# Down-projections of a split-precision transformer: two three-step products against one 512-column and one 256-column step

## The reference

```
def swiglu_2(x, w_gate, w_up, w_down):
    return (jax.nn.silu(x @ w_gate) * (x @ w_up)) @ w_down
...
for l in range(DEPTH):
    h = rmsnorm(x, ffn1_norm[l])
    x = x + 0.5 * swiglu_2(h, ffn1_w_gate[l], ffn1_w_up[l], ffn1_w_down[l])
    ...                                    # mixer, output projection
    h = rmsnorm(x, ffn2_norm[l])
    x = x + 0.5 * swiglu_2(h, ffn2_w_gate[l], ffn2_w_up[l], ffn2_w_down[l])
return rmsnorm(x, final_norm)
```

## Time and profile before

| | |
|---|---|
| median of three runs | 1949.19 us |
| profiled execution, first to last instruction | 1945.9 us |
| TensorE busy | 1931.2 us, 99% |
| VectorE busy | 1431.5 us, 74% |
| ScalarE busy | 1019.8 us, 52% |
| mean granted TensorE clock | 0.999 |
| DMA queue of the weights | 48.0% of 16 engines |

### The profile page before, as it was taken

How to read it: one execution, slowest core, us unless ns; L and a number is a source line. 1 busy time by engine, 2 the same in 40 slices (tenths; PEclk the granted TensorE clock), 3 DMA queues, 4 the chain that set the end, 5 groups by cost and what they waited for, 6 DMA issues and landing times.

```text
span 1945.9 us, 42335 instructions
## 1 busy us (share of the span) xinstructions
PE 1931.2 (99%) x16150; PEld 1892.7 (97%) x16150; DVE 1431.5 (74%) x2591; ACT 1019.8 (52%) x1527; POOL 152.7 (8%) x192
## 2 busy tenths in 40 slices
PE   9999999999999999999999999999999999999998
PEld 8999989999999999899999999999999999999998
DVE  6774787987588768879978874667765775667763
ACT  4443687554455447865547443665445444565443
POOL 0001123000100011320010100000000000100000
PEclk9999999999999999999999999999999999999999
DMA  7454433545454544345553665445555555435554
GB/s 265 172 197 170 166 109 112 192 174 193 156 192 172 196 164 145 109 152 194 201 191 140 235 233 183 151 149 185 193 214 177 195 202 208 152 131 195 194 213 154
DMA packets 46830, 346.66 MB, mean 178 GB/s; under 512 B 5344, under 2 KB 6416, under 8 KB 9232
## 3 DMA queue, kind: packets, MB, share of 16 engines
q1 hardware_dynamic: 44416, 335.63, 48.0%
q0 software_dynamic: 2320, 9.74, 1.6%
HBM read 344.29 MB, written 1.07 MB: 177 GB/s over the span
## 4 chain that ended last, share of the span: by engine, by line
PE 91%; DVE 4%; ACT 2%; DVEq 1%; issue 1%; DMA 0%; ACTq 0%; SPq 0%; POOL 0%
PE ps L622 22%; PE ps L623 22%; PE ps L624 22%; PE ps L639 14%; PE ps L630 2%; PE ps L631 2%; PE ps L632 2%; DVE w_lo L1996 1%; PE ps L1162 0%; DVE pj L2465 0%; DMA h<-in_hidden 0%; DVE cst L2486 0%; PE ps L1197 0%; DVE pj L2462 0%; ACT scratch L1669 0%
## 5 line engine op out<-in xcount | busy, mean ns | idle before, releaser
L1996 DVE TENSOR_TENSOR w_lo<-raw,w_hi 128x1024 fp32r<-128x1024 f32 (+1 forms) x582 | 749.3, 1313 | 151.1 <-ACT w_hi L1300 91.5
L622 PE MATMUL ps<-x_hi,w_lo 128*128 128x256 f32 (+3 forms) x2208 | 622.1, 282 | 1.5 <-DVE x_lo L2087 0.6
L624 PE MATMUL ps<-x_hi,w_hi 128*128 128x256 f32 (+3 forms) x2208 | 615.1, 279 | 0.0
L623 PE MATMUL ps<-x_lo,w_hi 128*128 128x256 f32 (+3 forms) x2208 | 614.8, 278 | 0.0
L1297 ACT ACTIVATE w_hi<-raw 128x1024 fp32r<-128x1024 f32 x454 | 466.3, 1052 | 92.5 <-PE ps L639 49.0
L622 PE MATMUL ps<-hid_hi,w_lo 128*128 128x256 f32 (+1 forms) x1536 | 431.5, 281 | 0.1
L624 PE MATMUL ps<-hid_hi,w_hi 128*128 128x256 f32 (+1 forms) x1536 | 430.2, 280 | 0.0
L623 PE MATMUL ps<-hid_lo,w_hi 128*128 128x256 f32 (+1 forms) x1536 | 429.8, 280 | 0.0
L622 PEld LDWEIGHTS ps<-x_hi,w_lo 128*128 128x128 f32 x2208 | 414.9, 188 | 6.4 <-issue 4.2
L623 PEld LDWEIGHTS ps<-x_lo,w_hi 128*128 128x128 f32 x2208 | 415.0, 188 | 0.5
L624 PEld LDWEIGHTS ps<-x_hi,w_hi 128*128 128x128 f32 x2208 | 414.6, 188 | 0.0
(11 more groups left out here) (351 smaller groups left out, 2315.3 us busy)
## 6 DMA issues: line engine op xcount, KB each, us to landing
raw<-in_w_up SPq DMA_DIRECT2D x176, 1024.0 KB, 4.8
raw<-in_w_down SPq DMA_DIRECT2D x64, 1408.0 KB, 6.0
raw<-in_w_in SPq DMA_DIRECT2D x36, 1024.0 KB, 4.8
raw<-in_w_out SPq DMA_DIRECT2D x16, 1024.0 KB, 4.8
cst<-row_copy POOLq DMA_DIRECT2D x2, 1088.0 KB, 8.5
raw<-in_w_up SPq DMA_DIRECT2D x4, 512.0 KB, 7.2
cst<-in_consts POOLq DMA_DIRECT2D x1, 1537.5 KB, 6.5
prm<-in_prm POOLq DMA_DIRECT2D x2, 690.0 KB, 7.2
```

The costliest lines, as they stand in the source:

```text
L622: mm(dst, low, xa, start=first, stop=False)
L623: mm(dst, high, xb, start=False, stop=False)
L624: return mm(dst, high, xa, start=False, stop=last)
L1996: v.tensor_tensor(dst, src, high.bitcast(F32), ALU.subtract).then_inc(lo_done, 1)
```

## The change

In stages 4 to 7 the two products with the high weights become one step. The moving operand of that step is both halves of a chunk, 2 x 256 = 512 columns, and its output is a whole PSUM bank: columns 0 to 255 get high by high, columns 256 to 511 high by low. The step with the low weights (256 columns, high activations) adds into columns 256 to 511. Each f so takes two steps in place of three, with the same number of columns, 768.

VectorE adds the bank's two halves to `h` in two instructions with a drain between (`resid_halves`), in place of one.

Order and places differ by stage (`WIDE`): in stage 5 the wide step comes first for each f, in 4, 6 and 7 second (but for f = 0, where it clears the bank). In stages 4 and 5 the halves lie where they lay; in stage 6 the high and low chunks alternate, so that the 512 columns are contiguous; in stage 7 the low half lies 16 elements earlier. The two hidden buffers become one allocation, 32 elements longer. Stages 0 to 3 are as they were.

```diff
-        HID_HI_W, HID_LO_W = NF * T1 + 4 * LINE, NF * T1 + LINE
+        HID_HI_W, HID_LO_W = NF * T1 + 4 * LINE, NF * T1 + 3 * LINE
...
-        def hid_of(T):
+        FIRST_HIGH, SECOND_HIGH, ADJACENT = "high weights first", "high weights second", "halves side by side"
+        WIDE = {4: (SECOND_HIGH, 0), 5: (FIRST_HIGH, 0), 6: (ADJACENT, 0), 7: (SECOND_HIGH, LINE)}
+
+        def hid_halves(q):
+            kind, more = WIDE[q]
+            if kind == ADJACENT:
+                return hid_all[:, HID_HI_T2:HID_HI_T2 + 2 * NF * T2].rearrange("p (k e t) -> p e k t", k=NF, e=2)
+            span = HID_HI_W + HID_LO_T2 - HID_HI_T2 - more
+            both = hid_all[:, HID_HI_T2:HID_HI_T2 + 2 * span].rearrange("p (e w) -> p e w", e=2)
+            return both[:, :, 0:NF * T2].rearrange("p e (k t) -> p e k t", k=NF)
...
             def down(q, turn0, resid, T):
+                def wide(j, f, high, low):
+                    kind, _ = WIDE[q]
+                    halves, bank = hid_halves(q)[:, :, f, :], ps[:, 4 + j, :]
+                    pair = bank.rearrange("p (e t) -> p e t", e=2)
+                    if kind == FIRST_HIGH or f == 0:
+                        mm(pair, high, halves, start=f == 0, stop=False)
+                        return mm(bank[:, T2:2 * T2], low, halves[:, 0, :], start=False, stop=f == NF - 1)
+                    mm(bank[:, T2:2 * T2], low, halves[:, 0, :], start=False, stop=False)
+                    return mm(pair, high, halves, start=False, stop=f == NF - 1)
...
+                                if q in WIDE:
+                                    last = wide(j, f, high, low)
+                                else:
+                                    last = three(ps[:, 4 + j, 0:T], high, low, ha[:, f, 0:T], hb[:, f, 0:T],
+                                                 f == 0, f == NF - 1)
...
+            def resid_halves(m, bank):
+
+                c = slice(m, m + 1) if isinstance(m, int) else bass.ds(m, 1)
+                dst = h[:, c, T1 - T2:T1]
+                v.tensor_tensor(dst, dst, ps[:, bank:bank + 1, T2:2 * T2], ALU.add)
+                dve.drain()
+                v.tensor_tensor(dst, dst, ps[:, bank:bank + 1, 0:T2], ALU.add).then_inc(resid_ready, 1)
...
-                        resid(alpha, it * 2 + j, 4 + j, T)
+                        resid_halves(it * 2 + j, 4 + j)
...
-                        resid(1.0, it * 2 + j, 4 + j, T2)
+                        resid_halves(it * 2 + j, 4 + j)
```

More of the change, by code:

```diff
@@ L234, in build @@
         small = sb("small", [P, 96])
-        HID_HI_W, HID_LO_W = NF * T1 + 4 * LINE, NF * T1 + LINE
+        HID_HI_W, HID_LO_W = NF * T1 + 4 * LINE, NF * T1 + 3 * LINE
         HID_HI_T2, HID_LO_T2 = 3 * LINE, LINE
-        hid_hi_all = sb("hid_hi", [P, HID_HI_W], F32R)
-        hid_lo_all = sb("hid_lo", [P, HID_LO_W], F32R)
+        hid_all = sb("hid", [P, HID_HI_W + HID_LO_W], F32R)
+        hid_hi_all, hid_lo_all = hid_all[:, 0:HID_HI_W], hid_all[:, HID_HI_W:HID_HI_W + HID_LO_W]
         SCRATCH = HID_HI_W + HID_LO_W
@@ L305, in cat1, with hid_of @@
             return x_of(T)
-        def hid_of(T):
+        FIRST_HIGH, SECOND_HIGH, ADJACENT = "high weights first", "high weights second", "halves side by side"
[7 more added lines that the diff above has]
+            return both[:, :, 0:NF * T2].rearrange("p e (k t) -> p e k t", k=NF)
+        def hid_of(T, q):
+            if q in WIDE:
+                both = hid_halves(q)
+                return both[:, 0, :, :], both[:, 1, :, :]
             return (hidt_hi, hidt_lo) if T == T2 else (hid_hi, hid_lo)
@@ L813, in down @@
             def down(q, turn0, resid, T):
-                ha, hb = hid_of(T)
+                ha, hb = hid_of(T, q)
+                def wide(j, f, high, low):
[7 more added lines that the diff above has]
+                    return mm(pair, high, halves, start=False, stop=f == NF - 1)
                 def turn(it):
@@ L826, in turn @@
                                 col = u * W_WIDE + c * P
-                                last = three(ps[:, 4 + j, 0:T], w_hi[:, j, col:col + P], w_lo[:, j, col:col + P],
-                                             ha[:, f, 0:T], hb[:, f, 0:T], f == 0, f == NF - 1)
+                                high, low = w_hi[:, j, col:col + P], w_lo[:, j, col:col + P]
+                                if q in WIDE:
+                                    last = wide(j, f, high, low)
+                                else:
+                                    last = three(ps[:, 4 + j, 0:T], high, low, ha[:, f, 0:T], hb[:, f, 0:T],
+                                                 f == 0, f == NF - 1)
                             last.then_inc(unit_used, 1)
@@ L1335, in first_cast @@
                 src = pj[:, j:j + 1, 0:T] if it == 0 else prod[:, j:j + 1, 0:T]
-                fn(hid_of(T)[0][:, f, 0:T], src, ACT.Copy).then_inc(first_casts, 1)
+                fn(hid_of(T, 2 * DEPTH)[0][:, f, 0:T], src, ACT.Copy).then_inc(first_casts, 1)
             def up(q, turn0, T, crossing=False, place=TIGHT):
@@ L1517, in pair @@
                     f = slice(f, f + 1) if isinstance(f, int) else bass.ds(f, 1)
-                    fn(hid_of(T)[0][:, f, 0:T], prod[:, j:j + 1, 0:T], ACT.Copy).then_inc(cast_done, 1)
+                    fn(hid_of(T, q)[0][:, f, 0:T], prod[:, j:j + 1, 0:T], ACT.Copy).then_inc(cast_done, 1)
                     if width == W_WIDE:
```

## The result

| | before | after |
|---|---|---|
| median of 4 runs each, us | 1949.30 (1948.94 to 1949.48) | 1958.76 (1957.47 to 1960.05) |
| profiled execution: span, us | 1945.9 | 1955.7 |
| windows of stages 4 to 7, us | 59.84 each | 62.02, 62.17, 62.01, 62.17 |
| end of stage 7 to the end of the span, us | 8.6 | 9.1 |

The changed kernel is slower: ratio 1.005, 95% interval 1.0036 to 1.0064. The forecast was 1943.6 us and the range ended at 1952.0. Executions of every kernel here, the one before included, fall into two groups some 2.7 us apart (the four of before lie in one of them, those of the change in both), a difference that arises in the first network, so spans and stretches are better compared than two medians.

What follows compares the result with a forecast made beforehand. The prediction took the pace of TensorE's steps to bound the kernel: profiled span 1945.9 - 6.1 (steps) + 0.5 (tail) = 1940.3 us, plus 3.3 for runs over span, gives 1943.6 us; range 1939.0 to 1952.0.

Steps and rivals of the forecast that it cites:

- Part 1: Stages 4 to 7: the 256-column low-weight step stays at 113.3 ns, with 111 below and 125.0 above.
- Part 2: Stages 4 to 7: wide step 218 ns, so an f takes 331.3 ns for 340.0, 6.1 us less in all.
- the sign of being wrong: Stages 4 to 7: the forecast is wrong if the wide step costs 227 ns or more.
- Part 5: DMA and places in stages 4 to 7: no transfer becomes late, hidden chunks at other addresses cost nothing.
- rival B: Stages 4 to 7: two streams far apart clash at unlucky places, f takes 348.6 ns, 1955.8 us; chance 0.13.
- the sign that the prediction gave for places: Stages 4 to 7: windows differing by more than 0.3 us would mean that order and place matter.
- The argument from the number of steps: Stages 4 to 7: same columns, a third fewer steps and weight loads, 704 times; each nanosecond off an f is 0.70 us.
- Rivals A and C: Stages 4 to 7: A, surplus goes with columns, 1949.7 us, chance 0.2; C, both steps lose the surplus, 1939.8, chance 0.12.
- A rule weighed again: TensorE steps: the skill's N / 2.4 GHz plus 2.5 ns makes the new f 325 ns; the trace before disagreed, 340.0 against 327.5.
- Part 4: VectorE's second addition: 0.50 us for each block, hidden inside stages and at ends of 4 to 6, +0.5 us after stage 7.
- rival D: Ends of stages 4 to 6: hand-over late, up to 1 us lost in each of three stages, 1946.6 us; chance 0.05.
- The base of the sum: Whole kernel: runs are 3.3 us above the profiled span, so a span of 1940.3 becomes 1943.6 us.

Runs made afterwards that it cites:

- experiment 4: Changed kernel put back to three 256-column steps and one addition, hidden halves at four other places: 353.4 to 357.3 ns per f, against 340.0 before.
- experiment 1: Changed kernel with other steps in each stage: wide step split in two 60.00 us, low-weight step into the lower half 62.17, two wide steps 462.2 ns per f.
- Experiment 2: Changed kernel with both steps of each f at one length, chunks alternating: 125.6 ns a step at 272 columns, 146.4 at 320, 176.4 at 384, 231.1 at 512.
- experiment 6: Changed kernel with the low weights alone moved (gap 0, 1 or 3 lines for 2), several high places: 341.4 to 353.2 ns per f; spans 1973.8, 1983.1, 1984.4 us.
- experiment 9: Three steps at the places of before, plus one more VectorE addition and drain for each block: 1950.76 us against 1946.86 for the kernel before, ratio 1.001.
- experiments 3: Changed kernel with low weights first in all four stages and hidden halves at other pairs of places: 346.6 to 351.9 ns per f.

## Why the prediction was wrong, step by step

**Part 1, the low step, priced "as before, 113.3 ns": wrong.** It measured 119.5 beside a wide step, 6.2 more. The reading of the instruction was right (same weights, same chunk, same load), and the conclusion was not: 113.3 ns was the price of a step at a place found for it, in a sequence of 256-column steps. The same 256-column steps cost 117.8 to 119.1 on average one to three lines away (experiment 4), and 118 to 120 at the old place for four steps behind a wide one (experiment 1).

**Part 2, the wide step at 218 ns: the failed step of the sum.** It measured 232.9, over the 227 that the prediction named as the sign of being wrong. The nearest row was a plain fp32 step that streams its columns twice; its 2 ns of surplus did not carry over to an fp32r step of 512 columns. The bound from the other side, the pace of the 272-column stages, gave 235.3 and was the good row: it was fp32r, in the same loop, with the same loads. That it came so close is in part luck: scaled by columns it makes the surplus 22 ns, and two wide steps in a row have 17.8. Experiment 2 shows that the 272-column step belongs to the common case (12 to 18 ns of surplus from 272 to 512 columns) and the 256-column step is the exception (7.6 in the same layout). I took the common case for the odd one.

**The two together:** 232.9 + 119.5 = 352.4 ns for an f instead of the forecast 331.3. The stages were to become 6.1 us shorter and became 9.0 longer, 15.1 us. In spans the miss is 1955.7 - 1940.3 = 15.4: these 15.1, the 1.1 of the unchanged stretch and -0.8 of the opening. Against the median it is 15.2.

**Part 5, "the hidden chunks are written by the same instructions at other addresses: nothing": half wrong.** The sentence behind it, that the trace can't say what places do, was right and should have weighed more. All four stages of before stood at one set of places, so their agreement was one observation and not four. Against rival B I counted "all four 256-column stages are free of it", which was this one observation. In the change itself the places tried made little difference (0.16 us): all have the high chunks at line 3. So the sign that the prediction gave for places, stages more than 0.3 us apart, stayed away although places matter; over all gaps and lines they are worth from 341.4 to 353.3 ns for an f of the wide form.

**Rival B: nearly right in size and right in sign, its mechanism wrong in one half and open in the other.** It gave the wide step 235.3 ns and a slower kernel. Streams far apart are not the cause: the contiguous 512 columns of stage 6 and of experiment 2 cost as much. A clash of reads at unlucky places is not excluded (below). And it left the low step at 113.3, so the time it gave, 1955.8, was still 3 us short.

**The argument from the number of steps was right, and it was not what decided.** At four equal places the wide form saves 3.3 to 10.3 ns per f (experiment 4). The change traded three steps at 1 to 2 ns above their floor for a form that can't use these places. Rivals A and C fall: the surplus neither went with the columns (6.7 would have become 13.4, it became 19.6) nor vanished.

**A rule weighed again.** The wide steps measure 227.6 to 236.7 ns on average over a stage and the 256-column ones 113.3 to 121.2. The Trainium skill (TensorE: Matmul & The Clock Gate, section "Back-to-back issue gap") has 215.8 and 109.2 by its formula, which it gives for the gap of an isolated matmul; that is below every fp32r row here, and only the plain fp32 steps of the earlier trace rows, 215 ns, agree. The same page (section "Step-by-step: what each phase is for") has the streaming operand and the weight load read through independent ports; experiments 4 and 6, where 16 elements more or less for one of the two change the pace, are hard to fit with the reading that they never disturb each other, though no run here has one without the other.

**Part 4, the second addition: right.** Forecast 0.5 us at the end, measured 0.5, in the change and by itself in experiment 9. The three hand-overs stayed hidden, so rival D falls. The room at the end of stage 4 was 1.3 us (chunk 7 ready 3.45 us after the stage's end, taken after 42 x 0.1133 = 4.76), where I had worked out 0.84.

**Part 5, the DMA: right.** No transfer became late: TensorE is busy for the whole of the four windows, and a unit of `w_down` takes 6.0 us to land before and after.

**The base of the sum: 1.5 us off.** I added 3.3 us to the span, as the difference between the runs' median and the profiled span. Where span and time belong to one execution the difference is 1.8 (1957.48 and 1955.7). The profiled span of before with this 1.8 makes 1947.7, below all its runs, so that execution was not one of them.

**What stays open.** Why 113.3 ns at lines 3 and 379 with a gap of two, and why 227.6 + 113.8 at one place with a gap of one, is not explained. The pace changes when the columns move and the weights stay (experiments 3 and 4) and when the low weights move and the columns stay (experiment 6). A clash of the two reads fits that, but no run has columns streamed without a load beside them, so it is not shown. Nor is it known what a wide step leaves behind that slows the next four. Nearly 40 different wide stages were tried and none is under 340.0; whether a place exists that is, isn't known. The 1.1 us in the unchanged stretch comes with every changed kernel whose stretch was read, wide steps or not; its cause was not tested.

## What to carry to other kernels

A pace that equals its floor in a tuned kernel may be owed to addresses: price a new form by the untuned rows (here the 272-column stages), and before you give up a tuned sequence, move the old one by 16 elements and see what its steps cost without the luck. Four stages that share one layout are one observation. To compare two forms, compare them at the same places, and then each at its best.

## What was unexpected of the hardware

- The pace of a step of 256 fp32r columns with a 128 x 128 weight load beside it depends on where its operands lie, in steps of 16 elements or less: three of them take 340.0 ns at one place and 350.1 to 357.3 at the five others tried. Moving the low weights alone by 16 elements slows the up-projection's steps from 113.4 to 118.2 ns.
- One 512-column step among 256-column ones takes 226 ns itself, and the four steps behind it 118 to 120 ns in place of 113.
- From 240 columns down the pace hardly falls: 112.5 ns at 240, 111.7 at 192. From 256 to 272 columns at the same places it jumps from 114.3 to 125.6.
- Where every f has one, a 512-column step costs 227.6 to 236.7 ns on average over a stage, and the 256-column step next to it 113.8 to 121.2.
- Writing across column 256 of a PSUM bank, or to both halves in turn, costs nothing (114 ns; 60.00 us a stage).
